# Feed-forward stage: GpSimd makes the rests of the value tiles as well as those of the down tiles, VectorE keeps the gate tiles

## What is computed

```python
def conv_ffn(h, w_up, taps, conv_b, w_down, rows):
    a, g = jnp.split(h @ w_up, 2, axis=-1)           # value and gate, 2816 channels each
    g2 = g.reshape(bsz, rows, 64, f)                 # 256 tokens as a grid of 4 rows of 64
    gc = lax.conv_general_dilated(g2, taps[:, :, None, :], (1, 1), 'SAME', ..., feature_group_count=f)
    gc = gc.reshape(bsz, t, f) + conv_b              # 3 x 3 depthwise convolution
    return (a * jax.nn.gelu(gc, approximate=False)) @ w_down
```

## Time and profile before

| | us |
|---|---|
| median of 3 runs | 2168.83 |
| lowest and highest | 2167.55, 2168.96 |
| span of the profiled execution | 2164.4 |
| feed-forward loop and its ends, in that span | about 1940 to 2149 |

### The profile page before, as it was taken

The page is one execution under the profiler, slowest core; times in us unless marked ns, Lnnn a source line. Parts: engine busy times, 40 slices in busy tenths (PEclk is TensorE's granted clock), DMA queues, the critical chain, the costliest instruction groups (busy, mean ns, idle before and its releaser), DMA issues. The chain is left out here.

```text
span 2164.4 us, 34599 instructions
## 1 busy us (share of the span) xinstructions
PE 1935.6 (89%) x11448; PEld 1618.6 (75%) x11448; DVE 1311.8 (61%) x2074; ACT 942.5 (44%) x1308; POOL 663.3 (31%) x346
## 2 busy tenths in 40 slices
PE   7999878988788996689999999999997887689996
PEld 5988767977682335579999999999996665448885
DVE  2485676322216679976666666666666426739997
ACT  4556525434440217754444444444444462225553
POOL 5887516773550016720000000000000753203332
PEclk9999989998899998999999999999998998899998
DMA  5554203452335550035555555555555430024442
GB/s 179 185 182 159 98 1 127 166 175 78 135 128 176 184 197 26 0 117 187 190 185 184 187 188 186 184 187 191 184 184 176 161 127 0 10 101 171 170 170 87
DMA packets 84812, 309.76 MB, mean 143 GB/s; under 512 B 9680, under 2 KB 9808, under 8 KB 84496
## 3 DMA queue, kind: packets, MB, share of 16 engines
q1 hardware_dynamic: 83232, 301.75, 40.4%
q0 software_dynamic: 1520, 7.21, 0.9%
HBM read 307.87 MB, written 1.05 MB: 143 GB/s over the span
## 5 line engine op out<-in xcount | busy, mean ns | idle before, releaser
L1345 ACT ACTIVATE weight_high<-weight_ring 128x1024 fp32r<-128x1024 f32 x436 | 461.0, 1058 | 342.5 <-PE banks L823 310.0
L705 POOL TENSOR_TENSOR weight_rest<-weight_ring,weight_high 128x1024 fp32r<-128x1024 f32 x180 | 446.2, 2481 | 194.1 <-PE banks L823 174.4
L2109 DVE TENSOR_TENSOR weight_rest<-weight_ring,weight_high 128x1024 fp32r<-128x1024 f32 x256 | 314.6, 1229 | 213.0 <-PE banks L823 206.5
L823 PE MATMUL banks<-a_high,weight_high 128*128 128x256 f32 x1088 | 267.4, 283 | 3.3 <-issue 3.3
L823 PE MATMUL banks<-a_rest,weight_high 128*128 128x256 f32 x1088 | 267.9, 284 | 0.0
L1345 ACT ACTIVATE arena<-banks 128x512 f32<-128x512 f32 (+3 forms) x272 | 167.8, 647 | 199.8 <-PE banks L823 192.1
L769 POOL DMA_DIRECT2D arena<-in_rows x1 | 0.5, 530 | 713.5 <-DVE gated_rest L2117 713.5
L823 PEld LDWEIGHTS banks<-a_high,weight_high 128*128 128x128 f32 x1088 | 208.8, 192 | 8.4 <-issue 3.5
L823 PEld LDWEIGHTS banks<-a_rest,weight_high 128*128 128x128 f32 x1088 | 209.3, 192 | 4.9
L823 PE MATMUL banks<-weight_high,gated_rest 128*128 128x512 f32 x512 | 201.0, 393 | 0.0
L823 PE MATMUL banks<-weight_high,gated_high 128*128 128x512 f32 x512 | 200.6, 392 | 0.0
(11 more groups left out here) (305 smaller groups left out, 3676.6 us busy)
## 6 DMA issues: line engine op xcount, KB each, us to landing
weight_ring<-in_stream SPq DMA_DIRECT2D x504, 512.0 KB, 3.2
arena<-in_stream SPq DMA_DIRECT2D x66, 512.0 KB, 3.2
residual<-in_x SPq DMA_DIRECT2D x2, 512.0 KB, 3.7
arena<-in_mem POOLq DMA_DIRECT2D x2, 512.0 KB, 4.6
arena<-in_keys POOLq DMA_DIRECT2D x1, 1024.0 KB, 5.1
arena<-in_ctx POOLq DMA_DIRECT2D x2, 512.0 KB, 6.3
scratch<-in_span POOLq DMA_DIRECT2D x1, 1024.0 KB, 5.2
out<-scratch SPq DMA_DIRECT2D x2, 512.0 KB, 2.7
```

The costliest lines, as they stand in the source:

```text
L705: nc.gpsimd.tensor_tensor(w_lo[:, e % 2, :], raw(e)[0], w_hi[:, e % 2, :], ALU.subtract).then_inc(S["rest_ready"], 1)
L823: ins = nc.tensor.matmul(out, lhsT, rhs, start=start, stop=stop, skip_group_check=True)
L1345: return nc.scalar.activation(out, in_, f, **kw)
L2109: tt(w_lo[:, e % 2, :], raw(e)[0], w_hi[:, e % 2, :], ALU.subtract).then_inc(S[ready], 1)
```

## The change

GpSimd also makes the rests of the value tiles, in the order of the stream: value rest, `hidden_rest`, down rest in each turn. VectorE's `split_rest` of the value tiles goes, before the loop and in it. A semaphore of its own, `ffn_value_lo_ready`, counts them; TensorE and ScalarE wait on it where they waited on `ffn_lo_ready` for a value tile. No transfer moves, no buffer changes, and the conditions of every subtraction (`hi_ready`, `hi_used`) stay the same.

```diff
-            def split_down(r, turn=None):
+            def ffn_rest(r, ready, turn=None):
                 e = F0 + r
                 n = 0 if turn is None else turn * 6
                 pool.wait_ge(S["hi_ready"], n + (e + 1))
                 pool.wait_ge(S["hi_used"], n + e)
                 nc.gpsimd.tensor_tensor(w_lo[:, e % 2, :], raw(e)[0], w_hi[:, e % 2, :],
-                                        ALU.subtract).then_inc(S["ffn_down_lo_ready"], 1)
+                                        ALU.subtract).then_inc(S[ready], 1)
...
+            ffn_rest(1, "ffn_value_lo_ready")
+            ffn_rest(3, "ffn_value_lo_ready")
             hidden_rest(("a0",), 0, 0)
+            ffn_rest(4, "ffn_down_lo_ready")
             with pool.Fori(0, (FC - 2) // 2) as i:
                 for u in range(2):
-                    split_down(4 + 3 * u, i)
+                    ffn_rest(6 + 3 * u, "ffn_value_lo_ready", i)
                     hidden_rest(("ga", 2 * u + 1), i * 2 + (u + 1), (u + 1) % 2, i)
-            split_down(64)
+                    ffn_rest(7 + 3 * u, "ffn_down_lo_ready", i)
             hidden_rest(("ae",), FC - 1, 1)
-            split_down(65)
+            ffn_rest(65, "ffn_down_lo_ready")
...
                 for u in range(2):
-                    channels(2 + 3 * u, ("ga", 2 * u), 3 + 2 * u, i)
-                    channels(3 + 3 * u, ("ga", 2 * u + 1), 4 + 2 * u, i)
+                    channels(2 + 3 * u, ("ga", 2 * u), "ffn_lo_ready", 2 + u, i)
+                    channels(3 + 3 * u, ("ga", 2 * u + 1), "ffn_value_lo_ready", 2 + u, i)
                     down(4 + 3 * u, u, u, i)
...
-                    split_high(F0 + 4 + 3 * u, i, 6, (S["ffn_lo_ready"], i * 4 + (3 + 2 * u)))
-                    split_high(F0 + 5 + 3 * u, i, 6, (S["ffn_lo_ready"], i * 4 + (4 + 2 * u)))
+                    split_high(F0 + 4 + 3 * u, i, 6, (S["ffn_lo_ready"], i * 2 + (2 + u)))
+                    split_high(F0 + 5 + 3 * u, i, 6, (S["ffn_value_lo_ready"], i * 2 + (2 + u)))
...
-            for r in range(2):
-                split_rest(F0 + r, "ffn_lo_ready")
+            split_rest(F0, "ffn_lo_ready")
...
             conv_channels(("g0",), 0, n0, 0, meanwhile=lambda: split_rest(F0 + 2, "ffn_lo_ready"))
-            split_rest(F0 + 3, "ffn_lo_ready")
             hidden_channels(("a0",), 0, 0, second=False)
             with dve.Fori(0, (FC - 2) // 2) as i:
                 for u in range(2):
                     conv_channels(("ga", 2 * u), i * 2 + (u + 1), i * (2 * per) + (n0 + per * (u + 1)), (u + 1) % 2, i,
                                   lambda: split_rest(F0 + 5 + 3 * u, "ffn_lo_ready", i, 6))
-                    split_rest(F0 + 6 + 3 * u, "ffn_lo_ready", i, 6)
                     hidden_channels(("ga", 2 * u + 1), i * 2 + (u + 1), (u + 1) % 2, i)
```

More of the change, by code:

```diff
@@ L429, in build @@
             mg_lo_ready a2_hi_ready a2_lo_ready co_hi_ready pq_hi_ready pq_lo_ready y_seeded a3_hi_ready
-            a3_lo_ready x3_hi_ready x3_lo_ready hi_ready hi_used lo_ready ffn_lo_ready ffn_down_lo_ready
+            a3_lo_ready x3_hi_ready x3_lo_ready hi_ready hi_used lo_ready ffn_lo_ready ffn_down_lo_ready ffn_value_lo_ready
             x1_hi_ready x1_lo_ready x2_hi_ready x2_lo_ready rest_ready column_ready square_made
@@ L1308, in _, with channels @@
             pe.wait_ge(S["act_ready"], 12)
-            def channels(r, job, count, turn=None):
-                split_channels(F0 + r, job, x3_hi, x3_lo, turn, 6, S["ffn_lo_ready"],
-                               count if turn is None else turn * 4 + count)
+            def channels(r, job, ready, count, turn=None):
+                split_channels(F0 + r, job, x3_hi, x3_lo, turn, 6, S[ready],
+                               count if turn is None else turn * 2 + count)
             def down(r, c, par, turn=None, last=False):
@@ L1326, in _ @@
             pe.wait_ge(S["x3_lo_ready"], 1)
-            channels(0, ("g0",), 1)
-            channels(1, ("a0",), 2)
+            channels(0, ("g0",), "ffn_lo_ready", 1)
+            channels(1, ("a0",), "ffn_value_lo_ready", 1)
             with pe.Fori(0, (FC - 2) // 2) as i:
                 for u in range(2):
-                    channels(2 + 3 * u, ("ga", 2 * u), 3 + 2 * u, i)
-                    channels(3 + 3 * u, ("ga", 2 * u + 1), 4 + 2 * u, i)
+                    channels(2 + 3 * u, ("ga", 2 * u), "ffn_lo_ready", 2 + u, i)
+                    channels(3 + 3 * u, ("ga", 2 * u + 1), "ffn_value_lo_ready", 2 + u, i)
                     down(4 + 3 * u, u, u, i)
-            channels(62, ("ge",), 43)
-            channels(63, ("ae",), 44)
+            channels(62, ("ge",), "ffn_lo_ready", FC)
+            channels(63, ("ae",), "ffn_value_lo_ready", FC)
             down(64, FC - 2, 0)
@@ L1713, in _ @@
             split_high(F0 + 2, rests=(S["ffn_lo_ready"], 1))
-            split_high(F0 + 3, rests=(S["ffn_lo_ready"], 2))
+            split_high(F0 + 3, rests=(S["ffn_value_lo_ready"], 1))
             with act.Fori(0, (FC - 2) // 2) as i:
@@ L1723, in _ @@
             ffn_gate(("ge",), FC - 1, 1)
-            split_high(F0 + 64, rests=(S["ffn_lo_ready"], 43))
-            split_high(F0 + 65, rests=(S["ffn_lo_ready"], 44))
+            split_high(F0 + 64, rests=(S["ffn_lo_ready"], FC))
+            split_high(F0 + 65, rests=(S["ffn_value_lo_ready"], FC))
             ffn_gelu(FC - 1, 1)
```

## The result

The changed kernel takes 2200.44 us, median of 4 runs (2200.29 to 2202.61), against 2168.61 for the kernel before in the same comparison. The ratio is 1.0147, 95% interval 1.0134 to 1.0161: slower, by 31.8 us. The forecast was 2200.0 us.

The account below looks back on a forecast made before the run. VectorE, partly standing behind GpSimd at the SBUF port, was taken to set the 9.25 us turn. Loop 28.8 plus 2.4 us ahead of it gave 31.2, added to the 2168.83 median: 2200.0 us, range 2176 to 2222.

Parts of the forecast that it names:

- The bound and its cause: Loop: VectorE sets the 9.25 us turn; about 2.2 us are VectorE standing behind GpSimd, 1.9 at tap 3.
- Who goes first: SBUF port: a waiting GpSimd instruction precedes VectorE's next; tap 7 goes before the value rest, tap 8 stands behind it.
- Ahead of the loop: Value rests r = 1 and r = 3, before the loop: about 0.85 and 1.6 us lost, sum 2.4 us.
- The turn: Loop: tap 8, held by the value rest, delays gelu and hidden_high; a turn grows 1.44 us, from 9.25 to 10.69.
- rival A: Loop: evacuation late too, hidden_rest passes tap 1, one more tap held; 2.23 us a turn, 2216 us; chance 0.13.
- The loop: Twenty value rests (r = 6 to 63) at 1.44 us each: 28.8 us lost.
- TensorE's clock: TensorE in the loop: busy about 79%, so nothing charged for a fall to the lower clock level.
- What was taken away: VectorE's value rest in the loop: 1.14 us come out once a turn; the 1.44 us growth is net of it.
- Rival C: Loop: VectorE and GpSimd don't exclude each other; TensorE bounds at 8.41 us a turn, 17 gained, 2152 us; chance 0.05.
- Rival B: Loop: value rest starts only after tap 8, hidden_rest 0.38 us later a turn; 10 us lost, 2179 us; chance 0.11.

Follow-up runs that it names:

- the kernel with the short rest: Kernel before, with VectorE's value rests in the loop cut from 1024 to 64 columns and nothing given to GpSimd: 2175.03 us, ratio 1.0031.
- the run with the evacuations first: Changed kernel, with ScalarE's two evacuations put ahead of the gelu in the loop: 2221.07 us, ratio 1.023.
- with tap 1 first: Kernel with value rests cut to 64 columns, where GpSimd's hidden_rest also waits until the next chunk's tap 1 is done: 2172.62 us, ratio 1.0022.

## Why the prediction was right, point by point

**The bound and its cause: right.** VectorE's stalls behind GpSimd, read off tap 3 before, are shown by taking them away (tap 3 at 0.41 us, 8.5 us a turn) and by adding one (1.89 us a turn). One thing was missing: the gate rest, TensorE and ScalarE form a second chain to tap 1, which was within 0.1 us of being the later one already. In the kernel before the second evacuation ends at 2034.62 and tap 1 starts 0.24 us behind; in the kernel with the short rest, where tap 1 waits for it, 0.15 us pass (2038.34 to 2038.49). It does not touch the forecast, in which VectorE gets slower; it decides what taking work away is worth.

**Who goes first: right, both ways.** The request of the value rest came at 2048.58 in the turn shown, before tap 7's end (2048.85), and tap 7 kept the port, tap 8 lost it. Ahead of the loop, with the gate rest late, the value rest of r = 3 passed tap 7, as forecast.

**The turn: 10.69 forecast, 10.78 measured.** Tap 8's hold was 1.89 us, as worked out. The 0.09 lie in two terms. From the gelu's end to line 2292 it is 0.19 us (2051.77 to 2051.96), where I took 0.15 from the expert stage. And tap 1 starts 0.02 us before the end of `hidden_high` (2041.88, 2041.90), where it was 0.08 before: it waits for the evacuation, the near tie that rival A rests on. Of these 0.06 the run with the evacuations first gives 0.03 back.

**The loop: 28.8 forecast, 31.3 measured** between first and last `hidden_high` (1954.5 to 2178.1 against 1951.2 to 2143.5, as the rows by tile give them). The difference is the 0.09 in twenty turns and one turn in rival A's order. In the first interval, 11.52 us, GpSimd's `hidden_rest`, down rest and value rest, and VectorE's taps 1 and 2 and gate rest, stand so:

```profile
1955.05 0.73 POOL L805 TENSOR_TENSOR hidden_rest<-arena,hidden_high 128x256 fp32r<-128x256 f32 x1 [2.05 <-DVE hidden_high L2293]
1955.88 2.39 POOL L799 TENSOR_TENSOR weight_rest<-arena,weight_high 128x1024 fp32r<-128x1024 f32 x1
1961.51 2.74 POOL L799 TENSOR_TENSOR weight_rest<-arena,weight_high 128x1024 fp32r<-128x1024 f32 x1 [3.24 <-PE banks L826]
...
1955.06 0.93 DVE L2279 SCALAR_TENSOR_TENSOR arena<-arena,cols 128x189 f32<-128x189 f32 x1 [0.16 <-ACT arena L1348]
1956.15 2.34 DVE L2279 SCALAR_TENSOR_TENSOR arena<-arena,cols 128x192 f32<-128x192 f32 x1 [0.16 <-DVE arena L2279]
1960.79 1.22 DVE L2112 TENSOR_TENSOR weight_rest<-arena,weight_high 128x1024 fp32r<-128x1024 f32 x1
```

0.01 us at the start of tap 1 decided which tap is the long one. The gate rest then ends late, at 1962.01, after the value rest has asked (1961.51), so the value rest passes tap 7 as well. Both parts of rival A's price are there: 11.52 − 9.35 = 2.17 us more than the first interval before, where A said 2.23. That all other turns took the cheaper order, by a few hundredths of a microsecond, is luck as far as the time is concerned: the forecast gave it 0.62 and could not have secured it.

**Ahead of the loop: 2.4 forecast, 2.0 measured.** The first `hidden_high` is 3.3 us later; 1.3 of these lie before the stage's first value rest (1944.61 on GpSimd, 1943.33 on VectorE before). The first gate rest already started 1.2 us later than before, at 1941.27, so that nearly all of this is not the change's. Of the 2.0, the value rest of r = 3 has 1.58 (1.6 forecast) and that of r = 1 has 0.43, where 0.85 was charged. The working charged it nearly twice: it let tap 1 end 0.43 us late, at 1945.95, and then started its successor at 1946.4, not 0.03 us behind that end.

**How near the hit is.** The loop and the part ahead of it measure 33.3 us together, where 31.2 were forecast. The spans of the two profiled executions differ by 34.3 (those 1.3 included), the medians by 31.8. The hit to 0.4 us is closer than the terms are, and that is luck. The table ahead of the prediction takes 4.4 us for launch and end. In the changed kernel the profiled run took 2200.53 us with a span of 2198.7, which is 1.8; so the profiled execution of the kernel before was some 2.6 us shorter than the median. The sum on the span would have been 2197.4, and only the one on the median gives 2200.0.

**TensorE's clock: right.** The granted clock of the changed kernel was 0.98 from 1940 to 1960 us and 1.00 in each 20 us from there to 2160.

**What was taken away: 1.14 us by its row, worth 0.36 in this order.** The sum was safe from this since it followed the end of tap 8 and the gelu behind it rather than subtracting. **Rival C's price was wrong**, and not only its premise. In C tap 3 stays long, so tap 1 to the end of the gate rest still takes 6.65 us (2025.61 to 2032.26), and the 2.5 to 2.6 us through TensorE and ScalarE to the next tap 1 follow: about 9.2 again, next to nothing gained. The kernel with the short rest bears this out, with 9.59 in the worse order and 9.48 with tap 1 first. TensorE's own turn, C's bound, is 8.5 and not 8.41 us. **Rival B's mechanism** holds when it is forced (2184.86 with 2179 priced): what it left out is that tap 1 stands behind the value rest too (1.22 us instead of 0.42).

Two slips without weight: the chances of the slower outcomes add up to 0.93 and that of no change is 0.02, where 0.92 and 0.03 are given; and the upper end of the range lies 6 us above rival A, not 2 to 3.

## What to carry to other kernels

Before work is moved from VectorE to an idle GpSimd, look for VectorE instructions that last several times as long as their own kind, and see whether each ends about 0.2 us after a GpSimd instruction: where they do, the move costs VectorE most of the GpSimd instruction (1.9 to 2.2 us here) to save its own (1.1), and the gain lies the other way: moving the down rests back to VectorE gained 16 us. Before functions on ScalarE are reordered, count the table loads. Where GpSimd must work, put it beside VectorE instructions with an input in PSUM, and by a wait if need be. And a removed instruction is worth only what the next chain leaves: follow who is late next to the end, since a few hundredths of a microsecond can change the order at a shared resource.

## What the runs showed of the hardware

- Two instructions that exclude each other hand over in turn: the one that waits goes ahead of the other engine's next. Where GpSimd's 128x1024 subtraction had waited, it ended 2.23 to 2.30 us after VectorE's instruction, and a held tap ended 0.21 to 0.22 us after GpSimd's (once 0.28), in every kernel here that has such pairs.
- The reported duration of an instruction contains its wait for the port: the same tap reads 0.42 or 2.33 us, and "busy" counts both. VectorE's busy time rose by 20.7 us with 22 instructions less.
- An engine that waits for the other's semaphore loses the port to an engine that has its next instruction queued: tap 1 came 0.16 us after `hidden_rest` and found the down rest in front of it.
- A table load takes 1.28 us, and the order of the functions decides how many there are and what they delay (11 or 21 in this stage). The Trainium skill ("ScalarE: Activation LUTs", section "What ACT_TABLE_LOAD costs") names 1283 ns for it, and the trace agrees. It adds 1380 ns of drain for each switch; the trace shows none beside the load, which starts 0.02 us after the evacuation's end (2049.60) and has the gelu 0.01 us behind it.
- TensorE's granted clock fell after it had stood idle for 3.2 us in the run with the evacuations first: 0.57 in the mean from 2054 to 2058 us. In the changed kernel, which waits 1.3 us a turn for `hidden_rest`, it was 1.00.
